# Moving three split operand tiles to other SBUF offsets in a two-block transformer kernel

## The reference

```python
# first block
h = rms_norm(x, g_pre_mix); proj = h @ w_in          # stick-breaking q, k, v; latents; rope key
o_sb  = stick_breaking_attention(...)                # 8 heads of 64
o_mla = mla_attention(...)                           # from the latents, through w_q_up and w_kv_up
x = x + rms_norm(concat(norm(o_sb), norm(o_mla)) @ w_o, g_post_mix)
u = causal_depthwise_conv(rms_norm(x) @ w_up, conv_w, conv_b)       # 2 * 2816 columns, 3 taps
x = x + rms_norm((gelu(gate) * val) @ w_down, g_post_ffn)
x = x + rms_norm(sigmoid(rms_norm(x) @ w_ple_gate + b) * (p @ w_ple), g_post_ple)
# second block
xn = rms_norm(x); proj = xn @ w_in_2                 # NSA q, k, v and gates, conv input, memory q, merge gates
merged = g0 * (o_nsa @ w_nsa_out) + g1 * (conv @ w_conv_out) + g2 * (o_mem @ w_mem_out)
h = x + merged @ w_out_2
out = h + (silu(hn @ w_gate_2) * (hn @ w_up_2)) @ w_down_2          # hn = rms_norm(h), 2816 columns
```

## Time and profile before

| | us |
|---|---|
| three timed runs | 896.15, 898.61, 898.70 (median 898.61) |
| span of the profiled execution | 892.3 |
| PE busy, PEld busy in it | 850.8, 815.1 |
| DVE, ACT, POOL busy in it | 656.3, 501.0, 321.8 |

### The profile page before, as it was taken

The page is one execution under the profiler, slowest core; times in us unless marked ns, Lnnn a source line. Parts: engine busy times, 40 slices in busy tenths (PEclk is TensorE's granted clock), DMA queues, the critical chain, the costliest instruction groups (busy, mean ns, idle before and its releaser), DMA issues.

```text
span 892.3 us, 16964 instructions
## 1 busy us (share of the span) xinstructions
PE 850.8 (95%) x6722; PEld 815.1 (91%) x6722; DVE 656.3 (74%) x981; ACT 501.0 (56%) x914; POOL 321.8 (36%) x148
## 2 busy tenths in 40 slices
PE   4999999999999999999999899999999999999998
PEld 3998889899999999798999789888999999999998
DVE  6894854898889996758799888965655676667573
ACT  6675656754565657765766574367545544434441
POOL 3743322212323324353655734332454232332320
PEclk8999999999999999999999999899999999999999
DMA  5743224344665656352646532222454456556541
GB/s 204 277 149 107 71 84 142 118 155 142 196 191 170 210 166 199 125 173 79 228 142 212 203 129 75 92 81 97 127 183 150 147 184 200 181 180 198 175 159 48
DMA packets 57246, 137.18 MB, mean 154 GB/s; under 512 B 6352, under 2 KB 27088, under 8 KB 57168
## 3 DMA queue, kind: packets, MB, share of 16 engines
q1 hardware_dynamic: 57168, 136.11, 46.9%
HBM read 135.03 MB, written 1.05 MB: 153 GB/s over the span
## 4 chain that ended last, share of the span: by engine, by line
PE 67%; DVE 18%; ACT 7%; issue 7%; DMA 1%; SPq 0%; DVEq 0%; ACTq 0%
PE PROD L615 14%; PE PROD L617 13%; PE PROD L616 13%; DVE YC L1926 5%; DVE wlo L1618 4%; ACT whi L1105 3%; PE PROD L677 3%; PE OP L817 2%; PE OP L615 2%; PE OP L617 2%; PE OP L616 2%; PE TP L617 2%; PE TP L615 2%; PE TP L616 2%; PE SC L615 1%
## 5 line engine op out<-in xcount | busy, mean ns | idle before, releaser
L598 POOL TENSOR_TENSOR wlo<-raw,whi 128x1024 fp32r<-128x1024 f32 x124 | 318.5, 2575 | 548.1 <-ACT whi L1105 523.1
L615 PE MATMUL PROD<-HA,whi 128*128 128x256 f32 x1080 | 313.0, 290 | 13.0 <-DVE HA L1647 6.2
L617 PE MATMUL PROD<-HA,whi 128*128 128x256 f32 x1080 | 308.1, 285 | 0.0
L616 PE MATMUL PROD<-HA,wlo 128*128 128x256 f32 x1080 | 308.1, 285 | 0.0
L1105 ACT ACTIVATE whi<-raw 128x1024 fp32r<-128x1024 f32 x252 | 262.0, 1052 | 50.9 <-PE PROD L617 29.0
L1618 DVE TENSOR_TENSOR wlo<-raw,whi 128x1024 fp32r<-128x1024 f32 x128 | 187.6, 1469 | 76.1 <-ACT whi L1105 76.0
L615 PEld LDWEIGHTS PROD<-HA,whi 128*128 128x128 f32 x1080 | 209.8, 194 | 16.1 <-DVE HA L1647 6.8
L616 PEld LDWEIGHTS PROD<-HA,wlo 128*128 128x128 f32 x1080 | 210.0, 194 | 0.6 <-issue 0.5
L617 PEld LDWEIGHTS PROD<-HA,whi 128*128 128x128 f32 x1080 | 209.7, 194 | 0.0
L1926 DVE SCALAR_TENSOR_TENSOR YC<-Y,CV,YC 128x255 f32<-128x255 f32 x88 | 66.9, 762 | 2.2 <-ACT YC L1329 0.7
L615 PE MATMUL OP<-HA,whi 128*128 128x256 f32 x200 | 57.6, 288 | 0.6 <-DVE KS L1703 0.5
(11 more groups left out here) (322 smaller groups left out, 1631.0 us busy)
## 6 DMA issues: line engine op xcount, KB each, us to landing
raw<-stream SPq DMA_DIRECT2D x197, 512.0 KB, 3.8
raw<-stream SPq DMA_DIRECT2D x144, 128.0 KB, 2.4
raw<-stream SPq DMA_DIRECT2D x28, 256.0 KB, 3.0
raw<-stream SPq DMA_DIRECT2D x4, 384.0 KB, 3.0
X<-xT SPq DMA_DIRECT2D x2, 512.0 KB, 5.6
out<-X SPq DMA_DIRECT2D x8, 128.0 KB, 2.0
KMEM<-memT SPq DMA_DIRECT2D x1, 512.0 KB, 5.3
VMEM<-memT SPq DMA_DIRECT2D x1, 512.0 KB, 6.1
```

The source lines that it names most:

```text
L598: nc.gpsimd.tensor_tensor(wlo[:, n % NSPLIT, :], raw[:, n % NRAW, :], whi[:, n % NSPLIT, :].bitcast(F32), ALU.subtract).then_inc(lo_pool, 1)
L615: nc.tensor.matmul(dst, wh, hi, start=start, stop=False, skip_group_check=True)
L616: nc.tensor.matmul(dst, wl, hi, start=False, stop=False, skip_group_check=True)
L617: last = nc.tensor.matmul(dst, wh, lo, start=False, stop=stop, skip_group_check=True)
```

## The change

Four unused tensors are declared between the tiles: 448 bytes per partition in front of `HA`, 128 in front of `HB`, 192 in front of `HL` and 256 behind `HL`. Together they are 1024 bytes, so all that is declared behind `HL` moves by 1024 bytes and keeps its place modulo 512 and modulo 1024. Nothing is read or written in them. No instruction, wait or loop is added, removed or moved.

```diff
         SQ = sb("SQ", [P, DC, S])
+        sb("before_ha", [P, 112])
         HA = sb("HA", [P, DC, 2 * S], F32R)
+        sb("before_hb", [P, 32])
         HB = sb("HB", [P, DC, 2 * S], F32R)
+        sb("before_hl", [P, 48])
         HL = sb("HL", [P, 4, 2 * S], F32R)
+        sb("behind_hl", [P, 64])
         KMEM = sb("KMEM", [P, MEMH, S])
```

## The result

| | before | after |
|---|---|---|
| median of five runs beside each other, us | 898.7 (896.15 to 900.51) | 889.17 (882.28 to 892.14) |
| ratio after / before | | 0.9903, 95% interval 0.9876 to 0.9929 |
| profiled execution: time, span, us | span 892.3 | 886.73, span 885.0 |

The change gains 9.5 us. The forecast was 21.1 us, and 889.2 lies above its range of 870 to 888 us. Medians, ranges and ratios are those of fast runs, which leaves out one execution of `after_relief` (2114.84 us) and one of `ha_only` (896.21 us).

A forecast was written before the change was run, and what follows sets the result against it. PE was taken to bound the kernel, by matmul count times start distance. Savings of 6.3 + 4.8 + 8.3 + 1.7 = 21.1 us were taken from 898.6, giving 877.5 us, range 870 to 888 us.

The forecast's parts named there:

- What bounds the kernel: Whole kernel: PE, busy 95% of the span, so the span is mainly matmul count times distance between starts.
- `HA`, 6.0 ns on 3,840 matmuls, 23.0 us: All matmuls moving `HA`: going from 384 to 320, the place of `ACTS`, saves 119.8 - 113.8 ns each, 23.0 us of PE time.
- `HB` and `HL`, -3 ns: 684 matmuls moving these tiles: -3 ns each taken, -2.1 us in all, with bounds of -8.9 and +4.1 us.
- `tm`, ACT and DVE at nothing: Some 160 `tm` products and the ACT and DVE instructions on the tiles: no cost; `tm` bounded at 1.0 us either way.
- Second feed-forward part, all of 6.3 us: 1,056 `HA` matmuls there, PE without idle time: the whole 6.3 us saving reaches the end.
- First feed-forward part, three quarters of 6.3 us: 1,056 `HA` matmuls there: some new PE waits come up, so 4.8 us of 6.3 reaches the end.
- it still fits: Tightest stretch of the first feed-forward part: PE would need 27.35 us, DVE at 97% still keeps up.
- DVE and the chains take most of it back: Rival, chance 0.17: first feed-forward part gives nothing, the rest passes on 0.6; 13.8 us gained, 884.8 us, stretch 883 to 893.
- more meetings with POOL: That rival's support, first feed-forward part: DVE taps lengthen beside POOL's subtraction, each further meeting costing DVE some 2.1 us.
- The rest, 0.8 of 10.4 and of 2.1 us, 10.0 us: Outside both feed-forward parts: 0.8 of `HA`'s 10.4 us, 8.3 us, and of 2.1 us for `HB` and `HL`, 1.7 us, arrives.
- The rule that the prediction set against the trace: Trainium skill, whole kernel: PE has two independent read ports and never waits on anyone, so offsets give zero, 898.6 us.

The follow-up runs named there:

- after_relief: Changed kernel, leaving out one of DVE's two taps per first feed-forward output and every second of 31 second-block convolution taps: 866.03 us, ratio 0.9667.
- ha_only: Changed kernel with only `HA` moved to 320, `HB` and `HL` left at 384: 888.6 us, ratio 0.9918 to the kernel before.
- before_inter: Kernel before, tiles at old places, DVE's scaling of the next `up` output put between its two taps in the first feed-forward part: 891.67 us, ratio 0.9958.
- second trace: Profile of the changed kernel run once more, nothing altered; that set measured 883.25 us, ratio 0.9866 to the kernel before.
- The relief: Half of DVE's taps in both convolutions left out, on both kernels: 885.64 us on the kernel before, 866.03 us on the changed kernel.
- the filled wait: Changed kernel, DVE's scaling of the next `up` output put between its two taps in the first feed-forward part: 882.35 us, ratio 0.9834 to the kernel before.
- second set of runs: The changed kernel timed once more, nothing altered, on another chip: 883.25 us (883.0 to 883.58), ratio 0.9866 to the kernel before.
- all320_inter: Changed kernel with `HA`, `HB`, `HL` all at 320 and DVE's scaling of the next `up` output between its taps: 879.61 us, ratio 0.9826 to before.
- all320: Changed kernel with `HA`, `HB` and `HL` all placed at 320: 881.54 us, ratio 0.9850 to the kernel before.
- w112: Against the kernel before, weights moved to 208 modulo 256 and split tiles to 64, so 112 bytes beyond the weights: 899.1 us, ratio 1.0043.
- m112: Against the kernel before, weights left at 128 modulo 256, all four moving tiles put at 240, 112 bytes beyond: 883.57 us, ratio 0.9870.

## Why the prediction was wrong

**What bounds the kernel: wrong in one part.** "The span is mainly a number of matmuls times the distance between their starts" holds for the second feed-forward part (all of the saving arrived) and failed for the first and, by `before_inter`, for the stretch from 505 to 674 us.

**`HA`, 6.0 ns on 3,840 matmuls, 23.0 us: right but for the second rate.** 6.5 ns where the faster rate holds (119.8 to 113.3), 5.2 on average over the kernel (119.8 to 114.6), so about 20.0 us. The missing 3 us are the stretches at 118 ns, which the trace of before did not give away, since nearly all of its `ACTS` rows were at 113 to 114.

**`HB` and `HL`, -3 ns: one right, one wrong.** `HB` gave 4.6 ns (2.9 in the second trace), inside the bounds. `HL` gave none (119.5 to 119.6): its new place is the old one modulo 256. On 204 matmuls that is 0.6 us.

**`tm`, ACT and DVE at nothing: right in size.** 512 columns against `HB` take 6 ns more, on some 48 of the 160 products, 0.3 us. DVE is busy 168.4 us in the first feed-forward part, 169.5 before.

**Second feed-forward part, all of 6.3 us: right.** It gave 6.9 (165.4 to 158.5).

**First feed-forward part, three quarters of 6.3 us: this step failed.** It gave 0.9 in place of 4.8, with PE's distances right: the share that reaches the end was wrong, since DVE's side and not PE held this part already. I counted DVE's 23.5 us of idle time there as room, and its 97% in the tightest stretch as "it still fits". That idle time belongs to DVE's loop and is not used up by sums that come from PE sooner. The waits of before said so: 1.1 us of DVE for PE, 76.5 us of ACT for DVE. The relief (6.9 us of the offset come through once DVE has less to do) and the filled wait (4.6 us from DVE's order alone, after the change) show it from two sides. The rival "DVE and the chains take most of it back" named this part and put it at nothing, and that is what came; 889.2 us lies in its stretch of 883 to 893. But its cause was another, more meetings with POOL, and DVE's busy time in the part did not grow (169.5 to 168.4 us); and the 7.5 us that it left to the rest did not come either, so its number is in part luck.

**The rest, 0.8 of 10.4 and of 2.1 us, 10.0 us: failed as well, and by more.** The profiled executions differ by 7.3 us of span, of which 7.8 lie in the two feed-forward parts: the rest gave nothing. By the medians it is 9.5 - 7.8 = 1.7 us, and with the second set of runs, 895.08 to 883.25, it is 11.8 - 7.8 = 4.0. So this term is off by 6 to 10 us, the first feed-forward part by 3.9. Its step was that PE's saving reaches the end but for a fifth. In the first trace it did so only from `gate` to `cmpk` (130.7 to 128.4 us, and 127.9 in the second trace).

One piece of the loss can be named. Ahead of `cmpk`, POOL and DVE both subtract weights. Before, DVE came first:

```profile
497.20 1.23 DVE L1618 TENSOR_TENSOR wlo<-raw,whi 128x1024 fp32r<-128x1024 f32 x1
...
497.34 3.35 POOL L598 TENSOR_TENSOR wlo<-raw,whi 128x1024 fp32r<-128x1024 f32 x1 [0.45 <-ACT whi L1105]
```

After, POOL came first, by 20 ns:

```profile
494.77 2.34 POOL L602 TENSOR_TENSOR wlo<-raw,whi 128x1024 fp32r<-128x1024 f32 x1 [0.30 <-ACT whi L1109]
...
494.79 3.40 DVE L1622 TENSOR_TENSOR wlo<-raw,whi 128x1024 fp32r<-128x1024 f32 x1
```

DVE's subtraction takes 3.40 us in place of 1.23, PE's stationary work waits 3.2 us for it (line 1001), and the stage is 20.9 us in place of 18.7. It is no accident of one run: seven traces with `HA` at a faster place, the changed kernel twice among them, have 3.4 us and 20.9, and the four of whole kernels in which its products run at about 120 ns have 1.2 and 18.7. (The one exception, `all320_inter`, has 18.6: there DVE's subtraction comes some 3 us earlier in the stage.) The clock is not the reason: in `all320` it is 1.00 in this stage. The Trainium skill has this as a rule ("SBUF — State Buffer", section "Who interferes with whom": a DVE instruction with two SBUF inputs contends with a GpSimd one that reads SBUF, for a port pair that is an exclusive lock, and the order of issue decides which of them blocks), and the rows agree: the first to start keeps its usual time, the second ends last.

PE's busy time fell by 18.7 us, 4.0 and 7.0 of it in the two parts, so 7.7 outside. Of these 1.7 to 4.0 reached the end and 2.2 went to this order, which leaves 1.5 to 3.8. In the first trace the lower clock between 129.8 and 133.2 us took some 1.6 of them. From 505 to 674 us PE's speed hardly counts, as `before_inter` showed above. With the taps halved the second block's attention up to `up2` went from 193.7 to 190.3 us by the offsets, and without from 196.2 to 196.0, so there too DVE's work stands in front; this is read from one trace of each, and how the remainder divides is not shown.

**The rule that the prediction set against the trace: the zero worked out from it did not come.** By the Trainium skill ("SBUF — State Buffer", section "Who interferes with whom": "PE and ACT never wait on anyone") the sum was zero. The offset alone moved the distance from 119.8 to 113.3 ns, in this kernel and in a kernel of matmuls only.

**What stays open.** Why the period is 256 bytes; what decides after a wait whether the stream goes at 113 or at 118 ns; whether it is the weights' place, 16 bytes off a multiple of 64, that holds the products of `w112` at 118 to 120, since no kernel varied that place alone; and what ACT's share in DVE's loop is.

## What to carry over

Idle time of the engine behind the matmuls is room only if that engine often waits for them: look in the list of waits of the stage for "consumer waits for producer", and if there is next to none (1.1 of 193 us here), cost a faster producer at nothing there and work on the consumer's loop first. Do so for every stage that the change touches: the larger miss here was the share taken for the rest. Where one instruction has two steady distances in a trace, compare the places of its operands modulo small powers of two, and measure the offsets by themselves in a small kernel before moving tiles in the large one. Where two edits lift two bounds of one stage, as the offsets and DVE's order here, try them together: in the first feed-forward part they gave 0.9 and 3.6 us alone and 5.5 in pair. By whole kernels this does not stand out (0.9903 or 0.9866, and 0.9958 alone; 0.983 in pair).

## What the runs showed of the hardware

- A float32r matmul of 256 columns with new weights each time started every 113.3 ns at best and every 120.0 at worst, at a granted clock of 1.00 (0.999 on the mean of each kernel of matmuls only), by where the moving operand stands beyond the stationary one modulo 256 bytes.
- At 64 and 192 bytes beyond the weights there are two steady rates, 113.3 and 117.8 ns. In the feed-forward parts of these traces one lasts until PE's next wait, through 337 matmuls in one case, and in `all320_inter` through a whole stage (164.6 us in place of 158.5).
- At 112 bytes all ten restarts were at 113.3 ns from the thirteenth matmul on, and the whole kernel ran so with weights at a multiple of 64 bytes (`m112`, `HA` at 113.9); with weights 16 bytes beyond one (`w112`) it was 118 to 120.
- Which of DVE and POOL starts a weight subtraction first, by 20 ns, decided over 2.2 us of a stage (DVE's took 3.40 us in place of 1.23).
- In stretches of 3.4 us with a granted clock of 0.50, the lower of its two levels (1.2 GHz), matmuls of this form started 213 ns apart in place of 114 to 120. One such stretch began behind a wait of PE of 3.2 us (498.5 us of the changed kernel's trace).
